# Two MLPs of a fused block on one Trainium2 core: where VectorE copies the first down tiles

## The reference

```python
D_FF_2 = 4 * D_MODEL          # 4096; D_MODEL is 1024

def _sqrelu_mlp(h, w_up, w_down):
    a = jax.nn.relu(jnp.einsum('bld,df->blf', h, w_up))
    return jnp.einsum('blf,fd->bld', a * a, w_down)

def second_block(...):
    hres = jnp.concatenate([meta, x], axis=1)          # 16 + 512 tokens
    for i in range(DEPTH_2):                           # 2
        h = _rmsnorm(hres, norm_g[i, 0])
        ...                                            # attention, or a short convolution
        hres = hres + _rmsnorm(m, norm_g[i, 1])
        h = _rmsnorm(hres, norm_g[i, 2])
        hres = hres + _rmsnorm(_sqrelu_mlp(h, w_up[i], w_down[i]), norm_g[i, 3])
    return hres[:, N_META:]
```

## Time and profile before

| what | value |
|---|---|
| median of 3 runs | 2006.25 us (2002.7 to 2010.27) |
| profiled execution, its own time | 2009.99 us |
| its span in the profile | 2007.5 us |
| mean granted TensorE clock | 0.975 |
| TensorE busy (PE), weight loads (PEld) | 1916.4 us (95%), 1691.4 us (84%) |
| VectorE busy | 1281.2 us (64%) |
| ScalarE busy | 784.2 us (39%) |
| GpSimd busy | 156.8 us (8%) |
| moved by DMA | 166.44 MB, mean 83 GB/s |

### The profile page before, as it was taken

One profiled execution on the slowest core, in us unless ns is written; L12 is line 12 of the kernel. 1 busy time (PEld: TensorE's weight loads), 2 busy tenths in 40 slices (PEclk: granted clock), 3 DMA queues, 4 the chain that ended last, 5 costly groups with the idle time before them and its releaser, 6 DMA issues.

```text
span 2007.5 us, 28677 instructions
## 1 busy us (share of the span) xinstructions
PE 1916.4 (95%) x11702; PEld 1691.4 (84%) x11702; DVE 1281.2 (64%) x1912; ACT 784.2 (39%) x1180; POOL 156.8 (8%) x127
## 2 busy tenths in 40 slices
PE   7999899999999999999999999999899988999996
PEld 6876777888888778899898899999899867898995
DVE  7676746434434676766649777776565468777764
ACT  4555433222213344444435344443422234444441
POOL 3000033000000220000012000000300130000001
PEclk9999989999999999999998999999899989999998
DMA  5130121222222231111111232222123222332321
GB/s 178 64 105 22 53 84 63 92 97 93 96 95 99 79 105 49 58 43 43 64 64 64 85 104 95 97 98 96 61 85 105 85 74 73 105 106 95 106 94 42
DMA packets 26077, 166.44 MB, mean 83 GB/s; under 512 B 3808, under 2 KB 4064, under 8 KB 6624
## 3 DMA queue, kind: packets, MB, share of 16 engines
q1 hardware_dynamic: 25232, 163.52, 23.8%
q10 hardware_dynamic: 720, 1.14, 0.2%
HBM read 162.55 MB, written 2.10 MB: 82 GB/s over the span
## 4 chain that ended last, share of the span: by engine, by line
PE 42%; DVE 7%; issue 1%; ACT 1%; ACTq 0%
PE ps L2524 6%; PE ps L2525 6%; PE ps L2526 6%; PE ps L2540 4%; PE ps L2539 4%; PE ps L2538 4%; PE ps L373 3%; PE ps L375 3%; PE ps L374 3%; DVE ps L530 1%; DVE h L543 1%; DVE z_lo L481 1%; DVE w_lo L355 0%; DVE arena L1888 0%; PE ps L2311 0%
## 5 line engine op out<-in xcount | busy, mean ns | idle before, releaser
L373 PE MATMUL ps<-z_hi,w_hi 128*128 128x512 f32 (+1 forms) x1008 | 368.4, 366 | 30.3 <-DVE z_lo L481 27.5
L374 PE MATMUL ps<-z_lo,w_hi 128*128 128x512 f32 (+1 forms) x1008 | 364.4, 362 | 0.0
L375 PE MATMUL ps<-z_hi,w_lo 128*128 128x512 f32 (+1 forms) x1008 | 362.9, 360 | 0.0
L355 DVE TENSOR_TENSOR w_lo<-w_raw,w_hi 128x2048 fp32r<-128x2048 f32 x95 | 217.8, 2293 | 90.5 <-ACT w_hi L344 90.4
L2524 PE MATMUL ps<-arena,w_hi 128*128 128x256 f32 (+2 forms) x768 | 247.5, 322 | 11.2 <-DVE acc L1854 10.7
L373 PEld LDWEIGHTS ps<-z_hi,w_hi 128*128 128x128 f32 x1008 | 195.1, 194 | 68.1 <-issue 22.6
L2525 PE MATMUL ps<-arena,w_hi 128*128 128x256 f32 (+2 forms) x768 | 247.7, 323 | 0.0
L2526 PE MATMUL ps<-arena,w_lo 128*128 128x256 f32 (+2 forms) x768 | 247.1, 322 | 0.0
L344 ACT ACTIVATE w_hi<-w_raw 128x2048 fp32r<-128x2048 f32 x95 | 180.9, 1905 | 146.7 <-PE ps L375 133.9
L375 PEld LDWEIGHTS ps<-z_hi,w_lo 128*128 128x128 f32 x1008 | 194.8, 193 | 29.9
L374 PEld LDWEIGHTS ps<-z_lo,w_hi 128*128 128x128 f32 x1008 | 195.0, 193 | 28.8 <-issue 0.7
(11 more groups left out here) (357 smaller groups left out, 4158.9 us busy)
## 6 DMA issues: line engine op xcount, KB each, us to landing
w_raw<-wstream SPq DMA_DIRECT2D x151, 1024.0 KB, 4.8
out<-h SPq DMA_DIRECT2D x8, 256.0 KB, 2.0
w_raw<-wstream SPq DMA_DIRECT2D x2, 512.0 KB, 6.1
h<-xT ACTq DMA_DIRECT2D x4, 256.0 KB, 6.5
h<-xT SPq DMA_DIRECT2D x4, 256.0 KB, 6.2
rope_cs<-pT SPq DMA_DIRECT2D x1, 512.0 KB, 5.5
acc<-pos SPq DMA_DIRECT2D x1, 256.0 KB, 10.5
acc<-lam SPq DMA_DIRECT2D x1, 128.0 KB, 9.9
```

The source lines that it names most:

```text
L355: dve.tensor_tensor(w_lo[:, slot, :], w_raw[:, slot, :], w_hi[:, slot, :].bitcast(f32), ALU.subtract).then_inc(wlo, 1)
L373: pe.matmul(dst, wh, zh, start=(k == 0), stop=False)
L374: pe.matmul(dst, wh, zl, start=False, stop=False)
L375: last = pe.matmul(dst, wl, zh, start=False, stop=(k == nk - 1))
```

## The change

In both MLPs:

```diff
@@ act_mlp (ScalarE)
                 both(1)
                 up_hi(FIRST, 1)
+                up_hi(FIRST, 0)
                 up_hi(FIRST, 2)
-                up_hi(FIRST, 0)
                 up_hi(FIRST, 3)
@@ dve_mlp, up_lo
-                        dve.wait_ge(s("us_hi"), since("us_hi", 3 * n + (part if i > FIRST else (part + 2) % 3) + 1))
+                        dve.wait_ge(s("us_hi"), since("us_hi", 3 * n + (part if i > FIRST else (1, 0, 2)[part]) + 1))
@@ dve_mlp (VectorE)
                 t_lo(0)
                 t_lo(1)
+                plain(2)
                 up_lo(FIRST, 1)
+                up_lo(FIRST, 0)
+                dve.wait_ge(s("t_lo"), since("t_lo", 4 * l + 2))
+                down(0, 0)
                 up_lo(FIRST, 2)
-                up_lo(FIRST, 0)
-                plain(2)
+                down(0, 1)
                 t_lo(2)
                 t_lo(3)
                 up_lo(FIRST, 3)
                 low(2, 0)
                 low(2, 1)
-                down(0, 0)
-                down(0, 1)
                 down_lo(1, 0)
+                dve.wait_ge(s("t_lo"), since("t_lo", 4 * l + 4))
                 down(0, 2)
@@ up_seven (TensorE)
-                    pe.wait_ge(s("us_lo"), since("us_lo", 3 * n + (1 if i > FIRST else 3)))
+                    pe.wait_ge(s("us_lo"), since("us_lo", 3 * n + (1 if i > FIRST else 2)))
```

## The result

| kernel | median | runs | ratio to before |
|---|---|---|---|
| before | 2005.83 us | 6 (2002.7 to 2010.27) | |
| changed | 1988.42 us | 6 (1987.48 to 1993.29) | 0.9919 (95%: 0.9905 to 0.9934) |

The changed kernel is faster by 0.8%. The ratio stands for 16.2 us less, with an interval of 13.2 to 19.1; the two medians themselves lie 17.4 us apart. The profiled execution took 1993.29 us around a span of 1991.5, the longest of its six runs; the one of before took 2009.99 around 2007.5, so the two differ by 16.7 us. Forecast were 15.0 us less and 1991.2 us.

The account below looks back on a forecast made before the run. TensorE, busy for 95% of the span, was taken as the bound. Wait and clock savings of 7.49 us (first MLP) and 7.56 (second), 15.05 taken as 15.0, from 2006.25 gave 1991.2 us; range 1986 to 1998.

Parts of the forecast that it names:

- The bound: TensorE waits 10.7 us in all at tile 2 of down block 0, both MLPs; what is removed arrives at the end.
- The path to the copy: VectorE's work ahead of down block 0's tile 0 copy falls from 8.67 to 2.94 us; second MLP keeps 0.18 us wait.
- The two terms of a wait: Tile 2 of down block 0: wait plus slow clock, 5.13 + 2.36 us first MLP, 5.73 + 1.83 second.
- the range: Whole kernel: 1986 to 1998 us, taking in the first two rivals and the median's own movement of 2 to 4 us.
- The added waits: VectorE's waits on `t_lo` for its own results: taken at 0, at most 0.15 us each.
- What is late next: VectorE reaches up block 3's evictions later against TensorE: 1.2 us second MLP, 0.4 first; cost taken as 0.
- The second rival: VectorE's lag exceeds the slack, TensorE waits at tile 2 of down block 1: 12.6 us gained, 1993.7 us; chance 0.08.
- the slack of 1.44: Second MLP, down block 1, tile 2: before, the copy released TensorE 1.44 us ahead of its getting there.
- The first, a clock that is not given back: After tile 1 of down block 0 clock stays 0.50; only waits gained, 10.9 us, 1995.4 us; chance 0.08.
- The third, that the copy comes no earlier or the gain returns elsewhere: Tile 0's copy stays late, or savings return where another engine had been waiting too: 2006 us; chance 0.07.
- The fourth, a lag that stays through the loop: VectorE's lag stays beyond the slack; 1 us wait in each of 26 later blocks, 2017 us; chance 0.03.

## Why the prediction was right

**The bound.** That what is taken from TensorE's wait arrives at the end was right: 15.07 us fewer in the two places, and 14.6 (0.9927), 14.4 (0.9928) and 16.2 us (0.9919) at the end, of about 2005. The three intervals all hold 15.0, and none of them is narrow enough to check the last us or two; the places do that.

**The path to the copy.** 2.94 us were worked out and 2.93 measured; the remaining wait was put at 0.18 us and is 0.16. In the first MLP none was forecast and none is there.

**The two terms of a wait.** 5.13 + 2.36 and 5.73 + 1.83 gave 7.49 and 7.56; the places show 7.49 and 7.58. The split between wait and clock was read from one execution. Over the executions that kept the waits the clock's term was 2.4, 1.3 and 2.5 us in the first MLP and 1.8, 1.7 and 2.0 in the second, so that 7.49 and 7.58 agree with the forecast to 0.02 us is in part luck: both sides use the same execution of before. The term is uncertain by about 1 us in the first MLP, and the range took that in without saying so. Why three measurements of the same change give 14.4 to 16.2 us was not isolated; the stretch ahead of the first place alone differs by up to 6.5 us between executions.

**The added waits.** Taken at 0, bounded by 0.15: the split ahead of the first takes 1.14 us with and without it.

**What is late next.** The first eviction of up block 3 was put 5.7 us behind the block's start and comes at 5.98 (1681.22 less 1675.24). That is 1.51 us more than the 4.47 of before, where 1.2 was forecast: the load took 5.1 us from issue to landing in place of 4.8, and VectorE waits 0.64 us for it where 0.3 was implied. The second rival named just this, a lag 0.3 us larger than worked out and so above the slack of 1.44, as its condition, and it was met here without the wait following. The step that the prediction lacks is that the lag shrinks on the way to the copy that matters, from 1.51 to 1.27 us. Most of this lies between a hidden low and the next eviction, 0.77 us from start to start before (1700.21 to 1700.98) and 0.61 after (1686.59 to 1687.20), so that a part of the lag went into what had been idle time before that eviction. That copy starts 14.56 us behind the first pass of up block 3, where it was 13.29. So the zero for this term was right by a margin that two errors of opposite sign left alone.

1689.80 and 0.84 release tile 2 of down block 1 at 1690.64, and TensorE gets there at 1690.81. The row (timeline of TensorE in the kernel after) has no wait:

```profile
1690.58 0.40 PE L2528 MATMUL ps<-arena,w_lo 128*128 128x512 f32 x1
1690.81 0.39 PE L2526 MATMUL ps<-arena,w_hi 128*128 128x512 f32 x1
```

The slack left is 0.17 us; 0.2 was forecast. It is thin: the work added on VectorE went through it.

**The rivals.** The first, a clock that is not given back, fell: 1.00 in both places, and 1.00 behind waits up to 2.59 us. The rule of the Trainium skill's page "TensorE: Matmul & The Clock Gate", section "A second HAM failure mode: psum-queue depth-cycling", speaks of frequent small idle times. The single waits of 0.34 and 1.12 us left the granted clock at 1.00; whether many of them in a row would make it fall, no run here shows. The second, a new wait one block later, didn't come about, but was made by 2.4 us of work. The third, that the copy comes no earlier or the gain returns elsewhere, fell with the copy's start and with the stretches behind the places, which are not longer than before by more than 0.2 us. The fourth, a lag that stays through the loop, fell even with the added work: TensorE waited for it at one block and not again.

**What was missed.** The prediction costed the exchange of the weight highs and TensorE's wait for two parts at nothing, and that was right. It never asked whether they are needed, nor the new order of the splits: the copies, with the evictions ahead of them, give all of the gain alone.

## What to carry to other kernels

Where an engine with a long list evicts PSUM, look for the eviction on which the matmuls' next tile hangs and put it directly behind the last thing that it depends on; here 7.5 us of other work stood ahead of it beside the evictions that it does depend on, and none of that was needed sooner. Price a wait of TensorE with what follows it: here waits of 5.0 to 5.7 us cost 6.4 to 7.8, one of 3.4 us cost 6.2, and one of 2.6 us cost 2.8. Then count what the evicting engine is late for, up to the next place at which it is waited for, and compare with the slack there: of 1.4 us, 0.17 were left. And ask of each part of a change whether the gain needs it.

## What the runs showed of the hardware that was not expected

The same wait on the same place (4.95 to 4.97 us of idle time) had slow clock behind it that cost 2.4 and 2.5 us in two executions and 1.3 in a third. An idle time of 2.59 us left the granted clock at 1.00, while behind one of 3.39 us it was 0.50, and the wait cost almost twice its length. And VectorE's wait on its own counter, with the result already there, costs nothing that the trace can show: 1.14 us with it and 1.14 us without.
